# The V projection of a two-layer encoder in seven products of half blocks, with weight sums made in DRAM and input sums made beside the first q and k

## The reference, cut to what matters

```python
qkv = (h @ w_qkv).reshape(bsz, rows, GRID_W, 3, N_HEADS, HEAD_DIM)
q = qkv[:, :, :, 0] * (HEAD_DIM ** -0.5)
k = qkv[:, :, :, 1]
v = qkv[:, :, :, 2]
...
scores = scores + bias[None].astype(jnp.float32)
p = jax.nn.softmax(scores.reshape(bsz, N_HEADS, GRID_W, kh * WIN_W), axis=-1)
...
return jnp.einsum('bhqrc,brqchd->bqhd', p, v_nb)
```

## Time and profile before

| | |
|---|---|
| time, median of 3 runs | 1047.38 us (1047.09 to 1047.47) |
| profiled execution | 1047.84 us, of which the span of instructions is 1045.9 us |
| PE busy | 1037.3 us, 99% |
| DVE, ACT, POOL busy | 822.5, 585.9, 96.9 us |
| DMA | 169.08 MB, mean 162 GB/s |

### The profile page before, as it was taken

How to read it: one execution, slowest core, us unless ns; L and a number is a source line. 1 busy time by engine, 2 the same in 40 slices (tenths; PEclk the granted TensorE clock), 3 DMA queues, 4 the chain that set the end, 5 groups by cost and what they waited for, 6 DMA issues and landing times.

```text
span 1045.9 us, 15397 instructions
## 1 busy us (share of the span) xinstructions
PE 1037.3 (99%) x6128; PEld 910.4 (87%) x6128; DVE 822.5 (79%) x1163; ACT 585.9 (56%) x828; POOL 96.9 (9%) x148
## 2 busy tenths in 40 slices
PE   9999999999999999999999999999999999999997
PEld 8888888988998998998888888888988988988986
DVE  5876688699899689688625767798799798698697
ACT  6222347564584574575535555647664673674675
POOL 2454001000000000000011000000000000000003
PEclk9999999999999999999999999999999999999999
DMA  7998568326745745632356323157056547547523
GB/s 246 366 377 301 143 167 252 105 46 207 207 134 172 180 134 171 180 104 80 101 156 191 111 86 112 61 169 294 1 121 196 167 131 201 152 131 202 151 51 111
DMA packets 34694, 169.08 MB, mean 162 GB/s; under 512 B 5504, under 2 KB 5632, under 8 KB 21824
## 3 DMA queue, kind: packets, MB, share of 16 engines
q1 hardware_dynamic: 22320, 105.42, 28.5%
q0 software_dynamic: 12016, 62.16, 24.7%
q10 hardware_dynamic: 288, 0.52, 0.2%
HBM read 125.40 MB, written 18.94 MB: 138 GB/s over the span
## 4 chain that ended last, share of the span: by engine, by line
PE 96%; DVE 1%; ACT 1%; DMA 1%; issue 0%; POOL 0%; POOLq 0%; ACTq 0%; DVEq 0%
PE bank L688 30%; PE bank L690 30%; PE bank L689 30%; PE bank L890 1%; PE bank L868 1%; PE bank L853 1%; PE bank L711 1%; DMA raw<-wo 1%; DVE w_l L1391 1%; PE bank L912 0%; ACT big L1060 0%; DVE xs L1538 0%; DVE a_l L1868 0%; ACT w_h L1032 0%; PE bank L917 0%
## 5 line engine op out<-in xcount | busy, mean ns | idle before, releaser
L1032 ACT ACTIVATE w_h<-big 128x1024 fp32r<-128x1024 f32 x210 | 221.7, 1058 | 216.4 <-PE bank L690 216.3
L688 PE MATMUL bank<-a_h,w_h 128*128 128x256 f32 (+1 forms) x892 | 294.8, 330 | 0.0
L690 PE MATMUL bank<-a_h,w_l 128*128 128x256 f32 (+1 forms) x892 | 292.9, 328 | 0.0
L689 PE MATMUL bank<-a_l,w_h 128*128 128x256 f32 (+1 forms) x892 | 292.8, 328 | 0.0
L1391 DVE TENSOR_TENSOR w_l<-big,w_h 128x1024 fp32r<-128x1024 f32 x210 | 252.2, 1228 | 21.8 <-ACT w_h L1032 21.8
L688 PE MATMUL bank<-w_h,hx 128*128 128x512 f32 x536 | 209.4, 391 | 0.0
L689 PE MATMUL bank<-w_l,hx 128*128 128x512 f32 x536 | 208.7, 389 | 0.0
L690 PE MATMUL bank<-w_h,hx 128*128 128x512 f32 x536 | 208.5, 389 | 0.0
L688 PEld LDWEIGHTS bank<-a_h,w_h 128*128 128x128 f32 x892 | 169.6, 190 | 15.6 <-issue 0.2
L690 PEld LDWEIGHTS bank<-a_h,w_l 128*128 128x128 f32 x892 | 169.6, 190 | 15.0
L689 PEld LDWEIGHTS bank<-a_l,w_h 128*128 128x128 f32 x892 | 169.6, 190 | 14.7 <-issue 0.2
(11 more groups left out here) (182 smaller groups left out, 1289.5 us busy)
## 6 DMA issues: line engine op xcount, KB each, us to landing
big<-blocks SPq DMA_DIRECT2D x56, 1024.0 KB, 5.4
raw<-weights SPq DMA_DIRECT2D x60, 512.0 KB, 4.5
big<-big POOLq DMA_DIRECT2D x30, 1024.0 KB, 7.2
bias_tiles<-big POOLq DMA_DIRECT2D x8, 632.0 KB, 9.8
big<-bias_tiles POOLq DMA_DIRECT2D x8, 632.0 KB, 4.1
big<-blocks POOLq DMA_DIRECT2D x4, 1024.0 KB, 24.0
raw<-wo_sums SPq DMA_DIRECT2D x8, 512.0 KB, 3.5
bias_tiles<-bias_rows POOLq DMA_DIRECT2D x48, 64.0 KB, 8.8
```

The costliest lines, as they stand in the source:

```text
L688: nc.tensor.matmul(dst, sh, mh, start=start, stop=False, skip_group_check=again)
L689: nc.tensor.matmul(dst, sh, ml, start=False, stop=False, skip_group_check=again)
L690: return nc.tensor.matmul(dst, sl, mh, start=False, stop=stop, skip_group_check=again)
L1032: nc.scalar.activation(wh_all[:, w % SLOTS, :], src, ACT.Copy).then_inc(w_hi, 1)
```

## The change

V is made in seven products too. The weight matrix of V gives its four blocks and T1 to T4, which are now made in DRAM along with those of the output matrix (`t_dram[0]` and `t_dram[1]`): twice the copies and accumulations, the first set whole before `add_sums(0)`. The ring of weights gets 14 units for V in place of 8. The input's sums S1 to S4 are made by DVE (`x_raw`, `v_round` on ACT, `v_rest`) while PE makes q and k of the first pair, which now stand between P2 and P4. The products' order is P1 P2 (q k) P4 P5 P6 P7 P3; P6 and P7 add into the banks of P1, P3 into those of P5. ACT copies an intermediate state of a bank (`v_got`), DVE adds others to it (`v_plus`). POOL's shifts wait for `v_add`.

```diff
-W_QK = W_V + 8
+W_QK = W_V + 14
...
+V_BANK = {"P1": 4, "P6": 4, "P7": 4, "P2": 6, "P5": 6, "P3": 6, "P4": 0}
...
+            def t1_made(i):
+                pool.wait_ge(negatives, 2 * i + 1)
+                pool.dma_start(t_dram[i][0], negated, accum_op=ALU.add).then_inc(t_made[i], 16)
+                pool.wait_ge(t_made[i], 16)
...
+            negative_in(0, "Y11")
+            for i in range(2):
+                for t, role in ((0, "Y12"), (2, "Y11"), (3, "Y21")):
+                    pool.dma_start(t_dram[i][t], sevens[i, Y_ROLES.index(role)]).then_inc(t_copied, 16)
+            pool.wait_ge(t_copied, 16 * 6)
+            t1_made(0)
+            negative_in(0, "Y22")
+            t2_made(0)
+            negative_in(1, "Y11")
+            t34_made(0)
             add_sums(0)
...
+            t1_made(1)
+            negative_in(1, "Y22")
+            t2_made(1)
+            t34_made(1)
...
             for half in range(2):
-                pool.wait_ge(v_got, 4 * (half + 1))
+                pool.wait_ge(v_add, 3 + half)
...
+            v_blocks("P2", range(2, 4))
+            unit(qk_unit(0, 0), q_bank(0), ready=a_place(2, 1))
+            unit(qk_unit(0, 1), k_bank(0))
+            v_blocks("P4", range(4))
+            pe.wait_ge(v_add, 1)
+            pe.wait_ge(v_lo, 1)
+            v_blocks("P5", range(4))
+            pe.wait_ge(v_copy, 1)
+            pe.wait_ge(v_lo, 2)
+            v_blocks("P6", range(4))
+            pe.wait_ge(v_copy, 4)
+            pe.wait_ge(v_lo, 3)
+            v_blocks("P7", range(4))
+            pe.wait_ge(v_copy, 3)
+            pe.wait_ge(v_lo, 4)
+            v_blocks("P3", range(4))
             for j in range(KT - 1):
                 scores(0, j)
+                if j == 0:
+                    pe.wait_ge(v_copy, 2)
+                    unit(qk_unit(1, 0), q_bank(1), ks=range(2))
...
+            hi(W_V + 14)
+            hi(W_V + 15)
+            v_got("P6", 0, 1)
...
+            v_plus("P7", 1, 1, 3)
+            v_plus("P7", 1, 0, 3)
...
+            v_plus("P3", 0, 1, 4)
```

More of the change, by code:

```diff
@@ L152, in wo_unit, with qk_unit, part_of @@
     return W_WO + 2 * WO_ORDER.index(name)
+def qk_unit(j, i):
+    return W_QK + 2 * j + i if j else W_V + 4 + i
+def part_of(w):
+    if W_V <= w < W_V + 16 and w - W_V not in (4, 5):
+        at = w - W_V
+        name = [p for p, first in V_UNIT.items() if first == at - at % 2][0]
+        return 0, PART[name], at % 2
+    if W_WO <= w < W_MLP1:
+        return 1, PART[WO_ORDER[(w - W_WO) // 2]], (w - W_WO) % 2
+    return None
 UNIT_OF_RING = [w for w in range(W_END) if ring_of(w) is not None]
@@ L467, in encoder @@
         s_lo = {name: sem(f"{name}_lo") for name in ("S1", "S2", "S4")}
[L468 to L472, removed]
+        seven_in = sem("seven_in")
+        negatives = sem("negatives")
+        t_copied = sem("t_copied")
+        t_stored = sem("t_stored")
+        t_made = [sem(f"t_made{i}") for i in range(2)]
+        v_copy = sem("v_copy")
+        v_add = sem("v_add")
+        v_sum = sem("v_sum")
+        v_hi = sem("v_hi")
+        v_lo = sem("v_lo")
         qk_hi = sem("qk_hi")
@@ L527, in _ @@
                     sp.dma_start(raw_all[:, 4 * P * k:4 * P * (k + 1)], wave[k]).then_inc(first_in[k], 16)
+            plain = [w for w in UNIT_OF_RING if part_of(w) is None]
             def ring_source(r):
                 w = UNIT_OF_RING[r]
[L532 to L536, removed]
+                if part_of(w) is None:
+                    return weights[plain.index(w)]
+                i, part, u = part_of(w)
+                at = slice(D * u, D * u + D)
+                return sevens[i, Y_ROLES.index(part)][:, at] if part in Y_ROLES else t_dram[i][int(part[1]) - 1][:, at]
             def load_ring(first, last):
@@ L644, in _, with negative_in @@
-            add_sums(0)
[L645 to L651, removed]
+            def negative_in(i, role):
+                pool.dma_start(negated, sevens[i, Y_ROLES.index(role)]).then_inc(seven_in, 16)
@@ L1289, in _ @@
+            v_round(1)
+            hi(W_V + 10)
+            hi(W_V + 11)
+            v_got("P4", 1, 0)
+            v_round(2)
+            hi(W_V + 12)
+            hi(W_V + 13)
+            v_got("P5", 1, 1)
+            v_round(3)
+            hi(W_V + 14)
+            hi(W_V + 15)
+            v_got("P6", 0, 1)
+            for w in range(W_V + 16, W_V + 20):
+                hi(w)
             for j in range(KT):
@@ new lines, in _ @@
+            v_rest(1)
+            dve.wait_ge(v_sum, 3)
+            x_raw(2, "X12")
+            lo(W_V + 10)
+            nc.vector.tensor_tensor(v_raw[2], v_raw[2], v_raw[1], ALU.add).then_inc(v_sum, 1)
+            lo(W_V + 11)
+            v_rest(2)
+            lo(W_V + 12)
+            v_rest(3)
+            for w in range(W_V + 13, W_V + 16):
+                lo(w)
+            v_plus("P7", 1, 1, 3)
+            v_plus("P7", 1, 0, 3)
+            dve.wait_ge(v_add, 3)
+            for b in tposed:
+                nc.vector.memset(b[:], 0.0).then_inc(banks_zero, 1)
@@ L2004 @@
     w_v = w_qkv[:, 2 * D:]
-    order += [wide(w_v, i, b) for b in range(2) for i in range(4)]
     for j in range(KT):
```

194 lines of the change are left out of this document (116 added, 78 removed).

## The result

| | before | after |
|---|---|---|
| median of 6 runs each | 1047.29 us (1046.23 to 1048.10) | 1066.18 us (1065.63 to 1070.58) |
| profiled span | 1045.9 us | 1064.0 us |
| matmuls on PE | 6128 | 6104 |

The ratio is 1.0188, with a 95% interval of 1.0171 to 1.0205: 18.9 us slower, where the forecast said 13.7. The time lies just above the stated range of 1052 to 1066.

A forecast was written before the change was run, and what follows sets the result against it. The prediction took PE, busy 99% of the span, as the bound. Its terms, -5.4 + 2.2 + 7.8 + 5.1 + 4.0 = +13.7 us, gave 1061.1 us, with a range of 1055 to 1066.5 and a wider one of 1052 to 1066.

The forecast's parts named there:

- P6 to P7: In V, PE waits while ACT copies P6's bank behind the rounding of P3's second unit: +2.2 us.
- bias tiles of the first pair: Ahead of the first transposes, tiles queued behind POOL's shifts land late and delay the first softmax: +7.8 us.
- T3 of matrix 0: Output matrix, before P7: T3 reaches SBUF at 169.5 us behind POOL's queued DRAM sums, PE waits: +5.1 us.
- T4 of matrix 0: Output matrix: T4 follows T3 by 5 to 6 us, nearly covered by P7's 5.4 us; no cost.
- low clock, two waits: PE returns at its lower clock after the waits for T3 and bias tiles: 2 us each, +4.0 us.
- (a): DRAM sums come in time, T3 landing by 164.4 us: 1054.0 us, chance 0.15.
- (c): POOL's queue runs further ahead, both large waits cost under 3.2 us, kernel faster; 1044.2 us at nothing; chance 0.06.
- (b): The first softmax doesn't wait, because its bias tiles land with its scores: 1051.3 us, chance 0.05.
- Rival (d): The output matrix's chain also makes T3 of matrix 1 late, 5 us more: 1066 us, chance 0.07.
- 4.8 to land: Bias tiles of the first pair land 4.8 us after issue, at 564.4 us, as in the earlier trace.
- PE then has three units split ahead of it: ACT's some 7 us standstill before the second sign change costs nothing; each unit holds 24 matmuls (5.4 us).
- the lower bound, 164.6: Earliest summed landing of matrix 0's T3 in SBUF, from quiet-stretch accumulation prices; 169.5 us was taken instead.

The follow-up runs named there:

- The two reordered runs: Changed kernel with bias tiles ahead of shifts, output-matrix copies behind matrix 0's T3/T4: with P6's copy first 1043.98 us; with P3 between P6 and P7 instead 1042.51 us.
- the fifth: Changed kernel with the output matrix's three copies moved behind T3 and T4 of matrix 0: 1056.69 us.
- the first experiment: Changed kernel with the bias tiles of the first two pairs loaded ahead of V's shifts, and the shifts' semaphore split by half: 1053.71 us.
- the shifts left out: Changed kernel without the seven shifts of V's second feature half, so later heads read wrong data: 1063.30 us.
- V's T3 and T4 behind: Changed kernel with V's T3 and T4 in DRAM made behind T3 and T4 of matrix 0: 1058.21 us.
- the bias tiles between: Changed kernel with bias tiles loaded between the first and second seven shifts of V, semaphore split by half: 1063.58 us, single run.
- the busy PE: Changed kernel with forty small unread matmuls in the pause ahead of the first transposes: 1065.47 us.

## Why the prediction was right in kind and 5 us short

By its own terms, as it put them, with what the distances of the trace after give (the first row is the count of matmuls times 0.227 us in both columns):

| term | forecast | measured |
|---|---|---|
| 24 fewer matmuls | -5.4 | -5.4 |
| P6 to P7 | +2.2 | +2.3 |
| bias tiles of the first pair | +7.8 | +11.1 |
| T3 of matrix 0 | +5.1 | +5.0 |
| sign change that comes late | 0 | +1.4 |
| T4 of matrix 0 (one cost with the clock behind T3, see below) | 0 | +1.2 |
| low clock, two waits | +4.0 | +3.3 |
| sum | +13.7 | +18.9 |

That the sum meets the medians' 18.9 us to a tenth is partly luck, since the terms are those of one execution. Its span is 18.1 us over that of before, and its start is 1.3 us shorter, so 19.4 us have to be explained there; the 0.5 us beyond the table are spread over many distances, each at most some 0.2 us too long.

**Right.** The direction, the three waits, their places and causes, and that the change's own work on DVE and ACT in V costs PE nothing: no run shows a wait within P1 to P5 of V. The two reordered runs end within 1 us of "fewer matmuls less the listed waits". That speaks against a cost of much more than that outside the list. The rivals (a) to (c) stood on a queue that runs further ahead than my sums; (a) and (b) are what the fifth and the first experiment make happen by reordering, at 1056.7 and 1053.7 us. Rival (d) has nearly the measured number, 1066, and not its mechanism: the list of waits after holds no wait at matrix 1. **Right by luck** is the size of the wait for T3, 5.0 for 5.1: the steps of the chain were off by up to 2.5 us and cancel.

**The step that failed, by 3.3 us: "4.8 to land", in the term of the bias tiles.** I took the landing from the earlier trace rows, where SP has nothing in the rings at the issue (its next load goes out later, at 554.70). In the changed kernel `lo` of two weight units stands directly ahead of V's last add on DVE, and each frees a place in the ring, so SP's loads go out at 562.39 and 563.51, ahead of the second shifts and of the tiles. I had moved the shifts and the tiles in time without asking what else is in the rings at the new time. In the changed kernel the landing is 8.1 us; with the loads held it is 4.7 and the wait 7.5, so the rest of that sum stands.

**The second: "PE then has three units split ahead of it".** True of the weights, and not the only thing that ACT makes. The stretch before the second sign change is where ACT also rounds the rest of the MLP's output, the input of `second(0)`. It stood still for 9.72 us (forecast: some 7), these roundings came after, and the k-steps of P1 waited for `hx`. The price was 1.4 us in this profile. It is not paid in every execution: of eight profiled runs with all six copies ahead of `add_sums(0)`, four have a wait for `hx` (the changed kernel 1.3, P6's copy first 1.7, the shifts left out 1.0, V's T3 and T4 behind 0.5 us), and those with the bias tiles first, the bias tiles between, the loads held and the busy PE show none in their lists. What tells them apart is when the second sign change runs: counted from the start of PE's 401st matmul, 41.4, 41.9, 42.2 and 44.0 us later in the four with the wait (0.5, 1.0, 1.3 and 1.7 us), and 39.8 to 40.9 us later in the four without. So the chain in DRAM has no slack there, and its own spread between executions, some 4 us, decides. What sets that spread was not tried.

**The third: T4 "nearly covered"** was 1.2 us. POOL's queue put 4.9 us between T3 and T4 (170.00 to 174.91), and two roundings and two splits of P4's units have to follow, while PE's P7 gave 5.4 us plus its low clock. The timeline of DVE shows one thing more in that path:

```profile
179.31 1.22 DVE L1495 TENSOR_TENSOR w_l<-big,w_h 128x1024 fp32r<-128x1024 f32 x1
```

This second split is what PE waits for. DVE was free from 178.4 us on but for a step of the layer norm that stands ahead of the split in its program and waits for two squarings on ACT (L1141), which stand behind the two roundings. That step puts 0.9 us into the path.

The wait for T4 and the low clock behind the wait for T3 are one cost and not two. Both lie in P7, between its first matmul and P4's, and that time is set by T4's path: 8.21 us in the changed kernel (172.46 to 180.67) and 8.2 to 8.3 in the six other profiled runs that wait for T3 and keep the order. In this profile 1.6 us of it is low clock and 1.2 us wait; in the six others 2.1 to 2.6 us is low clock and 0.2 to 0.7 us wait, and the sum is about 2.8 us in each. A higher clock in P7 would have been paid back as a longer wait.

**The clock** was a smaller error, the other way (3.3 for 4.0). Of the two waits only the one of the transposes costs its clock by itself (1.7 us for 2); for T3 the term of 2 and the 0 for T4 together stood for the 2.8 us above. The low stretch behind the transposes' wait is mostly pause: PE was back for 3.7 us of it. The Trainium skill (TensorE: Matmul & The Clock Gate, Part 1: The HAM clock gate) says that an idle PE falls to 1.2 GHz and earns the higher level by work. The trace agrees: 0.51 of the clock and 8.11 us behind the idle pause, 1.00 and 6.40 us behind the busy one.

**On turns between queues.** The Trainium skill (DMA: Bandwidth & Descriptors, Queues, rings and completion order) says that a DMA engine takes turns between the queues that have work; I weighed this for T3 only. Applied to the tiles it would have found the failed step: POOL's last shift took 7.3 us beside SP's loads and 2.8 without them. For T3 no run here separates it. Three of SP's loads were held back, but the fourth, 1 MB, went out at 151.99 and landed at 164.7 us, beside T4 of V in DRAM, which took 8.6 us for the 6.1 of the sum; T3 of matrix 0 came at 170.0, behind its own queue: from 148.15 to 174.91 that delivered four accumulations of 1 MB and the end of one load. The sum would have come near the lower bound, 164.6, by that rule, and only moving work out of POOL's queue brought it there.

**The ranges.** The prediction bounds the wait for T3 by 0.2 and 7.9 us and the clock by 0 and 3 us for each wait, but its own range takes 2 and 1.5 us as the lower ends; with 0.2 and 0 it would begin at 1051.5. Its terms reach up to 1066.5, above the end of the wider range, 1066, and the measured 1066.18 lies between the two.

## What to carry to other kernels

When a transfer moves in time, its price moves too: list what every other queue has in the rings at the new time, above all the loads that the neighbouring instructions themselves set free. When an engine is going to stand still, list everything that it makes in that stretch, not only what is first in line for the next engine. And where PE is 99% busy, a saving of 24 matmuls can be worth less than the place of a few DMAs in a queue: the seven products gained 3.0 us once the bias tiles stood ahead of the shifts, three copies behind T3 and P6's copy ahead of a rounding, and 4.5 us with another product in that copy's shadow instead.

## What the runs showed of the hardware

- **The low clock followed a wait of 2.1 us in five executions of eight, and mostly came after PE was back.** In the changed kernel the clock stayed at full speed behind the P6 to P7 wait (window 551.6 to 555.2). In the run with the bias tiles first, after the same wait (2.12 us, up to 550.21), PE went on at full speed for a microsecond and then was at the lower of its two levels for 3.5 us. The windows of each, changed kernel first (..., PEclk, DMA share, GB/s):

```profile
551.60:555.20 3.60, 3.29 (x14) 2.74 (x15) 0.64 (x1) 0.43 (x2) 0.00 (x0) 1.00 0.90 339
```

```profile
551.30:554.80 3.50, 3.50 (x10) 2.72 (x9) 0.00 (x0) 0.00 (x0) 0.00 (x0) 0.51 0.78 291
```

  In all, five of the eight profiled runs with that wait of 2.1 us had it (bias first, bias between, busy PE, loads held, shifts left out), each at a cost of 1.6 us; the two with 1.1 us did not. What decides it between like executions was not tried.
- **The first matmuls take up to 1.3 us longer in one execution than in another, for the same work.** The 31st matmul starts at 7.65 us of the span in the changed kernel and at 8.98 in the one before, and between the two in the ten other profiled runs. Before it stand small matmuls at 0.21 or 0.11 us and large ones at 0.43 or 0.23 us. The granted clock of the views is 1.00 from the start in both, so that this stands in the distances alone. It puts the profiled span of after 1.3 us nearer to that of before than the waits alone say.
- **In POOL's queue a copy of 1 MB in DRAM took 4.0 us and an accumulation 4.9 to 8.6.** Five copies behind the first took from 97.9 (89.4 + 8.5) to 117.8 us, 4.0 each; between T3 and T4 of matrix 0, one accumulation further in the same queue, lie 4.9 us, between T4 of V in DRAM and T3 of matrix 0 5.4, and between T3 and T4 of V in DRAM, beside a load of SP's, 8.6. The stretches differ in what SP loads beside them, so the prices are those of their places.
- **Small shifts within SBUF lost more, in proportion, than the tiles.** The last shift of 128 KB took 2.8 us to land without loads beside it and 7.3 us beside two loads of 0.5 MB, the tiles (632 KB) 4.7 and 8.1 us. How much of the 7.3 us is waiting behind the earlier shifts of its own queue was not tried.
